# Routing tokens to experts tile by tile inside the stage before, in a two-block transformer kernel on one core

## The chip, the core and the metric

One Trainium2 core runs the whole program once. The number is the device time of that launch in microseconds, the median of the runs shown. The engines are TensorE (PE, with its weight loads PEld), VectorE (DVE), ScalarE (ACT), GpSimd (POOL) and SyncE (SP, which here only issues DMAs).

## What is computed

512 tokens of width 1024 pass through a first block (three groups of dilated window attention and a retention branch, merged by gates, an `out` product, then a mixture of experts) and two layers of a second block. The change is all between the `out` product and the experts. In the reference, cut to that:

```python
h = h + mix                                   # mix = merged @ w_out
hn = rms_norm(h, norm_moe_w)
g_w, g_idx = top_k(softmax(hn @ w_group + b_group), 1)        # 8 groups
sel = (hn @ w_expert + b_expert).reshape(T, 8, 8)[group g_idx]
e_w, e_idx = top_k(softmax(sel), 2);  e_w = e_w / sum(e_w)
gate = g_w * e_w;  eid = g_idx * 8 + e_idx                    # 2 of 64 experts a token
y[token] = sum over its 2 experts e of gate * ((silu(x @ w1[e]) * (x @ w3[e])) @ w2[e])
```

Each w1, w3, w2 is 2048 KB, so the 64 experts read 192 such arrays.

## The kernel before

Every engine runs its own instruction list, and semaphores order them. Tokens lie in four tiles of 128 (`NT` = 4). Between stages all engines meet at a barrier (`next_stage`): PE, VectorE and ScalarE drain, POOL clears the stage's semaphores and opens the next stage (L254).

**The rest stage** (`rest_pe`, `rest_dve`, `rest_act`) follows one list of steps, `rest_steps`, which all three engines walk, each taking the steps that concern it. Its last eight jobs are the `out` product: half 0 of the columns for tiles 0 to 3, then half 1. A job is 24 matmuls in 8 chunks. VectorE adds the result to `h`. After half 1 of a tile, ScalarE sums the squares and VectorE writes the normed tile (L1307, L357). `x_turn` transposes that tile (L1060) and ScalarE copies it to `xnT`; `logits` multiplies it by the routing weights (L1047, 72 columns) into PSUM bank 7. `logits` of a tile stands one job behind its `x_turn`, the last two behind all jobs.

**The routing stage** (`route_pe`, `route_dve`, `route_act`) stands between two barriers. VectorE works on all four tiles at once: bias, best group, the two best experts in it, gates; then `either`, the 0/1 matrix of tokens by experts. TensorE multiplies it by a triangle and by ones, which gives each token's rank in its expert and each expert's count. An expert has 32 slots (`CAP`); ranks beyond that go to spilled blocks, whose experts come from a running sum over the counts. VectorE works out each assignment's slot, counting the spilled ones too (L1503 to L1523).

**The expert stage.** `experts_dve` begins with 0/1 matrices: `picks` (which token is in which slot of a quad of four experts) and `gated` (the same times the gate), for quad 0, then `picks` for quad 1, then `spilled_experts_dve`. TensorE gathers quad 0's tokens by matmuls of `xn` with `picks` (L1608), ScalarE copies them to `xT`. Then 64 turns, one for each expert e (`body`): TensorE does the gate product and the up product of e (L1618), the down product of e - 1 (L1634), a transpose of `gated` (L1725), a quarter of the gather for a later quad, the transposes of gate and up (L1625) and adds a finished tile's results (L1654). VectorE copies `up` out of PSUM (L1785), copies half of the down result, sums the transposed gate and up, multiplies them, and writes `picks` and `gated` for later quads.

**The loads** (`experts_sp`, L1570): eight slots of 2048 KB hold weights: slots 0 to 3 are the ring that also holds the units of the `out` product, slot 4 is `xnT`, slot 5 the routing weights' rows, slots 6 and 7 the upper end of `arena`. Eight loads are issued ahead; load (e, j) after that waits until PE has used its slot: `pair_used` counts in the gate/up and down products, `down_used` in the transpose of `gated`. The ninth load, (2,2), waits for `pair_used` 1, which expert 0's first up matmul gives; the tenth, (3,0), for `pair_used` 2, given by the first matmul of the gather in expert 0's turn; the eleventh, (3,1), for `down_used` 2, in expert 1's turn.

## Time and profile before

| | us |
|---|---|
| median of 3 runs (lowest, highest) | 2969.37 (2968.95, 2972.18) |
| profiled execution, its own time | 2969.08 |
| its span in the trace | 2967.3 |
| TensorE busy, share of the span | 2701.6, 91% |
| VectorE busy | 1305.7, 44% |
| mean granted TensorE clock | 0.966 |
| bytes by DMA | 572.19 MB |

The page cuts the span into 40 slices of 74 us. For each it gives the busy share of the engines, the granted TensorE clock (1.00 is 2.4 GHz, 0.50 is 1.2 GHz) and the GB/s moved by DMA. A mean over the span says little here, since stages have different limits; so the page is read for where a stage lies and the windows, waits and timeline for what limits it. Times in the trace are counted from the start of the span.

### The profile page before, as it was taken

Reading aid. Unit: us, or ns where it says so; the run is one execution under the profiler, and the core shown is the slowest. Engines: PE = TensorE matmul, PEld = TensorE weight load, DVE = VectorE, ACT = ScalarE, POOL = GpSimd, SP = SyncE. Lnnn points to the kernel's source line nnn. Section 1 sums busy time; section 2 is a strip of 40 time slices with the busy share of each in tenths; the row PEclk is TensorE's granted clock in tenths of the full one; section 3 lists DMA queues with packets and bytes.
Section 4 is the critical chain, followed back from the end, with each engine's and each line's share of the span. In section 5 each row is a group of like instructions: output and inputs, shape, how many; then the busy total and the mean of one; then the engine's idle time right before and its main releaser. Section 6 shows DMA issues by size and latency. Waiting matters only on the chain.

```text
span 2967.3 us, 35548 instructions
## 1 busy us (share of the span) xinstructions
PE 2701.6 (91%) x14188; PEld 1911.8 (64%) x14188; DVE 1305.7 (44%) x2359; ACT 873.9 (29%) x1643; POOL 705.8 (24%) x310
## 2 busy tenths in 40 slices
PE   7999999998788888888888789999999999899998
PEld 7987777887433333333333277688788776788787
DVE  4333745324533333333333366454443574644433
ACT  3333334332111111111111143543332344433332
POOL 4232233442000000000000122224445122234443
PEclk9999999999899999999999899899999999999999
DMA  3222211325799999999999721022322221122321
GB/s 141 85 89 104 72 64 66 103 85 206 300 426 428 427 429 428 429 428 430 428 429 427 331 83 57 29 86 85 105 94 85 98 79 57 57 86 86 98 102 71
DMA packets 126801, 572.19 MB, mean 193 GB/s; under 512 B 10705, under 2 KB 58193, under 8 KB 101329
## 3 DMA queue, kind: packets, MB, share of 16 engines
q1 hardware_dynamic: 121424, 561.08, 47.6%
q10 hardware_dynamic: 5248, 9.32, 0.9%
q8 instruction: 90, 1.47, 0.2%
q14 instruction: 39, 0.31, 0.0%
HBM read 566.12 MB, written 4.26 MB: 192 GB/s over the span
## 4 chain that ended last, share of the span: by engine, by line
PE 50%; DMA 24%; PEld 9%; DVE 7%; issue 4%; ACT 3%; POOL 1%; PEldq 1%; POOLq 0%; SPq 0%; ACTq 0%; DVEq 0%
PE ps L341 27%; DMA wide<-in_moe_w 17%; PEld ps L341 9%; PE ps L1217 7%; DMA arena<-in_moe_w 6%; PE ps L1634 4%; PE ps L1618 3%; PE ps L555 1%; POOL ring_r L310 1%; PE ps L1026 1%; PE ps L526 1%; ACT ring_r L298 1%; PE ps L541 1%; PE ps L2548 1%; PE ps L1017 1%
## 5 line engine op out<-in xcount | busy, mean ns | idle before, releaser
L310 POOL TENSOR_TENSOR ring_r<-ring,ring_r 128x1024 fp32r<-128x1024 f32 (+2 forms) x284 | 690.8, 2464 | 2182.2 <-ACT ring_r L298 2182.2
L341 PE MATMUL ps<-xnT_r,ring_r 128*128 128x512 f32 (+1 forms) x1664 | 494.8, 378 | 13.1 <-DVE xn_r L2510 7.2
L341 PE MATMUL ps<-ring_r,xnT_r 128*128 128x512 f32 (+1 forms) x1360 | 443.8, 397 | 11.8 <-POOLq L254 5.0
L341 PEld LDWEIGHTS ps<-xnT_r,ring_r 128*128 128x128 f32 x1664 | 307.9, 191 | 79.8 <-issue 14.6
L341 PE MATMUL ps<-ring_r,arena_r 128*128 128x512 f32 x1392 | 334.1, 397 | 3.1 <-issue 3.1
L341 PEld LDWEIGHTS ps<-ring_r,xnT_r 128*128 128x128 f32 x1360 | 288.0, 224 | 59.2 <-issue 16.3
L341 PE MATMUL ps<-xn_r,ring_r 128*128 128x512 f32 (+1 forms) x832 | 312.6, 376 | 0.0
L341 PEld LDWEIGHTS ps<-ring_r,arena_r 128*128 128x128 f32 x1392 | 261.4, 190 | 68.1 <-issue 13.7
L1618 PE MATMUL ps<-wide,arena 128*32 128x512 f32 x1536 | 203.3, 652 | 101.4 <-DMA wide<-in_moe_w 100.9
L298 ACT ACTIVATE ring_r<-ring 128x1024 fp32r<-128x1024 f32 (+2 forms) x284 | 270.6, 1024 | 82.0 <-DMA ring<-in_w_down 68.0
L1618 PEld LDWEIGHTS ps<-wide,arena 128*32 128x32 f32 x1536 | 42.3, 112 | 239.4 <-DMA wide<-in_moe_w 146.9
L1634 PE MATMUL ps<-wide,arena 128*32 128x512 f32 x768 | 182.7, 619 | 0.0
L2808 DVE SCALAR_TENSOR_TENSOR arena<-ps,arena 128x511 f32<-128x511 f32 x88 | 66.0, 749 | 257.6 <-ACT arena L2824 257.6
L341 PEld LDWEIGHTS ps<-xn_r,ring_r 128*128 128x128 f32 x832 | 158.7, 191 | 26.7
L1648 ACT ACTIVATE arena<-ps 32x512 f32<-32x512 f32 x64 | 37.5, 586 | 469.1 <-PE ps L1634 469.1
L341 PE MATMUL ps<-ring_r,h_r 128*128 128x512 f32 (+1 forms) x424 | 167.7, 396 | 0.0
L1785 DVE COPY arena<-ps 128x512 f32<-128x512 f32 x64 | 44.3, 692 | 276.8 <-PE ps L1618 267.4
L2824 ACT ACTIVATE arena<-ps,arena 128x512 f32<-128x512 f32 x88 | 60.7, 690 | 299.9 <-PE ps L341 299.9
L1608 PE MATMUL ps<-arena,xn 128*128 128x128 f32 x1024 | 126.5, 278 | 14.6 <-DVE arena L1669 14.6
L1634 PEld LDWEIGHTS ps<-wide,arena 128*32 128x32 f32 x768 | 47.9, 117 | 135.2 <-issue 135.2
L1608 PEld LDWEIGHTS ps<-arena,xn 128*128 128x128 f32 x1024 | 124.6, 198 | 14.8 <-DVE arena L1669 14.8
L1629 DVE TENSOR_REDUCE arena<-ps 128x128 f32<-128x512 f32 x128 | 82.5, 686 | 109.9 <-PE ps L1625 109.7
(352 smaller groups left out, 3625.5 us busy)
## 6 DMA issues: line engine op xcount, KB each, us to landing
wide<-in_moe_w SPq DMA_DIRECT2D x144, 2048.0 KB, 27.0
arena<-in_moe_w SPq DMA_DIRECT2D x48, 2048.0 KB, 27.3
ring<-in_w_in SPq DMA_DIRECT2D x25, 2048.0 KB, 8.2
ring<-in_w_up SPq DMA_DIRECT2D x22, 2048.0 KB, 8.7
ring<-in_w_down SPq DMA_DIRECT2D x10, 2048.0 KB, 8.0
ring<-in_w_out SPq DMA_DIRECT2D x6, 2048.0 KB, 8.4
ring<-in_w_ret_branch SPq DMA_DIRECT2D x2, 2048.0 KB, 8.8
attn_spill<-arena ACTq DMA_DIRECT2D x2, 1056.0 KB, 10.8
```

What stands on the lines that cost most here:

```text
L298: nc.scalar.activation(ring_r[:, 2 + q % 2, cols], unit_home(q)[:, cols], ACT.Copy).then_inc(half_high, 1)
L310: nc.gpsimd.tensor_tensor(ring_r[:, q % 2, cols], ring[:, q % 2, cols], ring_r[:, 2 + q % 2, cols].bitcast(F32), ALU.subtract).then_inc(ha ...
L341: ins = nc.tensor.matmul(bank, left, right, start=(start and k == 0), stop=(stop and k == 2))
L1217: ins = nc.tensor.matmul(ps[:, job_bank(n), 0:right.shape[1]], left, right, start=(x == 0), stop=(x == len(pairs) - 1))
L1608: return [nc.tensor.matmul(ps[:, into, (c - c0) * width:(c - c0 + 1) * width], xn[:, i, c * P:(c + 1) * P], E.picks[:, quad, i, 0:width], ...
L1618: res.append(nc.tensor.matmul(ps[g * CAP:(g + 1) * CAP, bank, :], xT[:, c, :], w[:, c, :], start=(c < 4), stop=(c >= KC - 4), tile_positio ...
L1629: return nc.vector.tensor_reduce(dst, ps[:, bank, :].rearrange("p (c g k) -> p c k g", c=FC, g=4), AX.X, ALU.add)
L1634: return [nc.tensor.matmul(ps[half * CAP:(half + 1) * CAP, DOWN_BANK, :], E.hT[:, c, :], w[:, c, half * BANK:(half + 1) * BANK], start=(c ...
L1648: return nc.scalar.activation(E.y[expert_rows(b), b // QUAD % 2, 0:BANK], ps[0:CAP, DOWN_BANK, :], ACT.Copy)
L1785: nc.vector.tensor_copy(E.up, ps[:, UP_BANK, :]).then_inc(Z.up_kept, 1)
L2808: link(nc.vector.scalar_tensor_tensor(out=acc[:, 1:], in0=bank[:, 0:S - 1], scalar=taps[:, 1:2], in1=acc[:, 1:], op0=ALU.mult, op1=ALU.add))
L2824: nc.scalar.activation(Y.acc[:, j % 2, s_], ps[:, UP_BANKS[n % 8], :], ACT.Copy, scale=Y.fconv[:, s_ * FB + j, FCONV - 1:FCONV]).then_inc( ...
```

## The change

- The barrier between the rest stage and routing, and the one between routing and the experts, are gone; so is the stage `route`. Ranks, logits and gathers are steps of the rest stage's list.
- `route_tile_dve` finds group and experts of one tile. It sets the logits of other groups to -1e30 and searches all 64, where before the logits of the best group were cut out first. `place_tile_dve` gives the tile's main slots from its rank alone (a rank of 32 or more gets a slot far away) and writes its `picks`.
- `first_gather_pe` gathers quad 0 by tile, accumulated over the tiles in four PSUM banks.
- Gates, `gated` and the `picks` of quad 1 are made at the start of the expert stage. The slots of spilled assignments (`all_slots_dve`) come behind VectorE's turn for expert 1, `spilled_experts_dve`, in two halves, behind its turn for expert 2.
- SP issues (2,0) and (2,1) behind the first two loads; (1,1) and (1,2) wait for the last tile's logits to be read instead of the barrier.

```diff
 rest_steps, for n over the jobs from 2 * NT:
+                last = n - job_at("out", 1, 0)
                 for c in range(len(REST[n][1]) // 3):
                     yield "chunk", (n, c)
+                    if last == 2 and c == 3:   yield "logits", 0
+                    elif last == 2 and c == 5: yield "route", 0
+                    elif last == 3 and c == 3: yield "logits", 1
+                    elif last == 3 and c == 5: yield "route", 1
+                    elif last == 3 and c == 6: yield "x_turn", 2
...
-                after = n - job_at("out", 1, 1)
-                if after >= 1:
-                    yield "logits", after - 1
-                if after >= 0:
-                    yield "x_turn", after
-            yield "logits", NT - 2
-            yield "x_turn", NT - 1
-            yield "logits", NT - 1
+                if 1 <= last <= 2:
+                    yield "x_turn", last - 1
+            rank 0, rank 1, logits 2, x_turn 3, route 2, rank 2, logits 3, place 0, place 1,
+            gather 0, gather 1, route 3, rank 3, place 2, gather 2, place 3, gather 3
...
+        def rank_pe(pe, i):
+            pe.wait_ge(Z.chosen, i + 1)
+            for j in range(i):
+                matmul(rank_of(i), table("ones"), G.either[:, j, :], start=(j == 0), stop=False)
+            matmul(rank_of(i), table("before"), G.either[:, i, :], start=(i == 0), stop=True).then_inc(Z.ranked, 1)
+            if i == NT - 1:
+                for j in range(NT):
+                    ins = matmul(ps[:, COUNT_BANK, 0:EXPERTS], table("ones"), G.either[:, j, :], ...)
+                ins.then_inc(Z.ranked, 1)
...
+        def route_tile_dve(v, link, i):
+            v.wait_ge(Z.logits_ready, i + 1)
+            tensor_tensor(G.logits, ps[logits of i], G.bias, ALU.add).then_inc(logits_taken, 1)
+            v.wait_ge(logits_taken, i + 1)
+            link(max(G.best, lg));  link(max_index(G.best_at, G.best, lg))
+            tensor_tensor(E.num[:, i, :], lg, G.best[:, 0:1], ALU.subtract)
+            link(tensor_copy(G.group, G.best_at[:, 0:1]))
+            link(scalar_tensor_tensor(masked, erow[:, 0:EGROUPS], G.group[:, 0:1], ones, is_equal, subtract))
+            link(scalar_tensor_tensor(G.masked, G.masked, -NEG, G.logits[:, EGROUPS:], mult, add))
+            link(max(G.top, G.masked));  link(max_index(G.top_at, G.top, G.masked))
+            ins = tensor_tensor(E.one[:, i:i + 1], G.top[:, 1:2], G.top[:, 0:1], subtract)
+            if i == NT - 1: ins.then_inc(Z.exp_asked, 1)
+            link(tensor_copy(E.e_at[:, i, :], G.top_at[:, 0:2]))
+            link(tensor_scalar(G.first_is, erow, E.e_at[:, i, 0:1], None, is_equal))
+            scalar_tensor_tensor(G.either[:, i, :], erow, E.e_at[:, i, 1:2], G.first_is, is_equal, add).then_inc(Z.chosen, 1)
+        def place_tile_dve(v, link, i):
+            v.wait_ge(Z.ranked, max(i + 1, 2))
+            for k in range(2):
+                ins = scalar_tensor_tensor(G.chosen[:, k], expert_row, E.e_at[:, i, k:k + 1], rank_of(i), is_equal, mult)
+            link(ins)
+            link(tensor_reduce(E.rank_at[:, i, :], G.chosen, AX.X, ALU.add))
+            link(G.over = (rank_at >= CAP) * FAR);  link(G.over += rank_at)
+            link(E.main[:, i, :] = e_at * CAP + over)
+            link(pick_dve(v, E.main, i, E.picks[:, 0]))
+            pick_second_dve(E.main, i, E.picks[:, 0]).then_inc(Z.picks_ready, 1)
...
         def experts_sp(sp):
             load_expert(sp, 0, 0, 0)
             load_expert(sp, 0, 0, 2)
+            load_expert(sp, 2, 2, 0)
+            load_expert(sp, 2, 2, 1)
             sp.wait_ge(unit_used, FIRST_UNITS)
             load_expert(sp, 0, 0, 1)
             load_expert(sp, 1, 1, 0)
-            sp.wait_ge(stage_open, STAGES_BEFORE_EXPERTS - 1)
+            sp.wait_ge(logits_taken, NT)
             load_expert(sp, 1, 1, 1)
             load_expert(sp, 1, 1, 2)
-            load_expert(sp, 2, 2, 0)
-            load_expert(sp, 2, 2, 1)
...
+        def first_gather_pe(pe, i):
+            pe.wait_ge(Z.picks_ready, i + 1)
+            if i == 0: wait_taken(pe, len(REST) - 1)
+            for q in range(QUAD):
+                for c in (2 * q, 2 * q + 1):
+                    ins = matmul(ps[:, q, (c % 2) * P:(c % 2 + 1) * P], xn[:, i, c * P:(c + 1) * P], E.picks[:, 0, i, :], ...)
+                if i == NT - 1: ins.then_inc(Z.gathered, 1)
...
         def experts_dve(v, link):
+            v.wait_ge(Z.ranked, NT + 1)
+            tensor_copy(E.count, ps[:, COUNT_BANK, 0:EXPERTS])
+            E.nearer = E.main - P;  link(E.ahead = E.main - 2 * P);  gates_dve(v, link)
             for i in range(NT):
-                pick_dve(v, E.slot, i, E.picks[:, 0])
-                link(pick_gated_dve(E.slot, i, E.gated[:, 0]))
-                pick_second_dve(E.slot, i, E.picks[:, 0]).then_inc(Z.picks_ready, 1)
+                link(pick_gated_dve(E.main, i, E.gated[:, 0]))
                 add_second_dve(i, E.gated[:, 0]).then_inc(Z.gated_ready, 1)
                 v.wait_ge(Z.gated_ready, i + 1)
-            for i in range(NT):
-                pick_dve(v, E.nearer, i, E.picks[:, 1])
+                link(pick_dve(v, E.nearer, i, E.picks[:, 1]))
                 pick_second_dve(E.nearer, i, E.picks[:, 1]).then_inc(Z.picks_ready, 1)
-            spilled_experts_dve(v, link)
...
             def body(it, b):
...
+                if first and e == 1: all_slots_dve(v, link)
+                if first and e == 2: spilled_experts_dve(v, link)
```

## Rows read from the trace of the kernel before

**Rows 1.** The page: GB/s in 40 slices, and the chain's shares by engine

```profile
GB/s 141 85 89 104 72 64 66 103 85 206 300 426 428 427 429 428 429 428 430 428 429 427 331 83 57 29 86 85 105 94 85 98 79 57 57 86 86 98 102 71
...
PE 50%; DMA 24%; PEld 9%; DVE 7%; issue 4%; ACT 3%; POOL 1%; PEldq 1%; POOLq 0%; SPq 0%; ACTq 0%; DVEq 0%
```

**Rows 2.** Windows: stretch, its us, busy of each engine, clock, DMA share, GB/s

```profile
780.00:790.00 10.00, 10.00 (x81) 4.76 (x77) 4.70 (x13) 2.04 (x5) 0.00 (x0) 1.00 0.95 370
...
800.00:1660.00 860.00, 730.80 (x4503) 312.05 (x4499) 317.12 (x660) 120.02 (x293) 0.00 (x0) 0.96 1.01 428
```

**Rows 3.** Waits of PE, 800 to 1660 us: total, times, longest

```profile
PE ps L1618 <- DMA wide<-in_moe_w: 97.7, 44, 3.0
```

**Rows 4.** Timeline of SP: start, duration, engine, line, operation, count

```profile
774.42 0.33 SPq L1570 DMA_DIRECT2D wide<-in_moe_w  x1
...
785.56 1.29 SPq L1570 DMA_DIRECT2D wide<-in_moe_w  x3
...
795.55 0.33 SPq L1570 DMA_DIRECT2D wide<-in_moe_w  x1
```

**Rows 5.** Timeline, end of the out product, idle before and its releaser in brackets

```profile
714.98 0.69 DVE L1307 TENSOR_TENSOR h<-h,ps 128x512 f32<-128x512 f32 x1 [2.31 <-PE ps L1217]
...
723.06 0.69 DVE L1307 TENSOR_TENSOR h<-h,ps 128x512 f32<-128x512 f32 x1 [3.56 <-PE ps L1217]
...
725.49 1.99 DVE L357 SCALAR_TENSOR_TENSOR xn<-h,small,rows 128x1024 f32<-128x1024 f32 x1
...
728.58 1.04 PE L1060 MATMUL ps<-cst,xn 128*128 128x128 f32 x8
...
730.36 2.00 PE L1047 MATMUL ps<-rows,xnT 128*128 128x72 f32 x16 [0.74 <-ACT xnT L1067]
```

**Rows 6.** Timeline of DVE in the routing stage and in the expert prologue

```profile
733.32 0.46 DVE L1447 TENSOR_TENSOR arena<-ps,small 128x288 f32<-128x288 f32 x1 [5.84 <-POOLq L254]
...
734.30 0.16 DVE L1455 FIND_INDEX8 arena<-arena 128x8 uint32<-128x8 f32 x1
...
748.10 0.20 DVE L1439 TENSOR_SCALAR arena<-arena 128x64 f32<-128x64 f32 x1
748.33 0.20 DVE L1440 TENSOR_SCALAR arena<-arena 128x64 f32<-128x64 f32 x1
...
754.99 0.16 DVE L1523 TENSOR_SCALAR small<-small 128x8 f32<-128x8 f32 x1
...
763.91 2.29 DVE L1529 TENSOR_TENSOR arena<-small,cst 128x2048 f32<-128x2048 f32 x1
```

**Rows 7.** Timeline of DVE: the first instruction of picks for tiles 0 and 1

```profile
756.11 0.29 DVE L1666 TENSOR_SCALAR arena<-small 128x128 f32<-128x128 f32 x1 [0.96 <-POOLq L254]
...
757.53 0.29 DVE L1666 TENSOR_SCALAR arena<-small 128x128 f32<-128x128 f32 x1
```

**Rows 8.** Timeline of PE: first gather, expert 0's products, gather in its turn

```profile
761.62 9.53 PE L1608 MATMUL ps<-arena,xn 128*128 128x128 f32 x64 [14.57 <-DVE arena L1669]
...
771.62 3.64 PE L1618 MATMUL ps<-wide,arena 128*32 128x512 f32 x32 [0.47 <-ACT arena L1645]
...
775.36 1.95 PE L1608 MATMUL ps<-arena,xn 128*128 128x128 f32 x16
```

**Rows 9.** Windows around the changes of the granted clock (column before DMA share)

```profile
308.00:309.00 1.00, 1.00 (x9) 0.89 (x9) 1.00 (x1) 0.00 (x0) 1.00 (x1) 0.85 0.00 0
...
735.00:736.00 1.00, 0.00 (x0) 0.00 (x0) 0.93 (x6) 0.22 (x1) 0.00 (x0) 0.69 0.43 147
...
741.00:746.00 5.00, 5.00 (x25) 5.00 (x25) 0.00 (x0) 0.00 (x0) 0.00 (x0) 0.50 1.01 429
...
765.00:766.00 1.00, 1.00 (x6) 1.00 (x6) 1.00 (x1) 0.38 (x1) 0.00 (x0) 0.50 0.00 0
766.00:767.00 1.00, 1.00 (x11) 1.00 (x10) 0.96 (x2) 0.00 (x0) 0.00 (x0) 0.95 0.00 0
```

**Rows 10.** Timeline of PE ahead of the fall at 308.7

```profile
305.54 2.98 PE L555 MATMUL ps<-arena,rows 64*128 64x64 f32 x16
```

More of the change, by code:

```diff
@@ L1133, in rest_dve @@
                     turn_tile_dve(v, k, Z.out_kept, M.mT[0], M.mT[1], Z.out_low)
+                elif what == "route":
+                    route_tile_dve(v, link, k)
+                elif what == "place":
+                    place_tile_dve(v, link, k)
         def gated_tile_dve(v, link, half, i):
@@ new lines, in gates_dve, with all_slots_dve @@
+        def gates_dve(v, link):
+            v.wait_ge(V.exp_ready, 1)
+            link(nc.vector.tensor_reduce(gates[:, :, 0], E.num, AX.X, ALU.add))
+            link(nc.vector.scalar_tensor_tensor(out=gates[:, :, 0], in0=E.one, scalar=1.0, in1=gates[:, :, 0], op0=ALU.add, op1=ALU.mult))
+            link(nc.vector.reciprocal(gates[:, :, 0], gates[:, :, 0]))
+            link(nc.vector.tensor_tensor(gates[:, :, 1], gates[:, :, 0], E.one, ALU.mult))
+        def all_slots_dve(v, link):
+            erow = table("expert_row")
+            link(nc.vector.tensor_scalar(E.further, E.count, -1.0, None, ALU.add))
+            whole_blocks(link, E.further, E.further)
+            link(nc.vector.tensor_scalar(E.further, E.further, 0.0, None, ALU.max))
+            link(nc.vector.memset(E.zeros, 0.0))
+            link(nc.vector.tensor_tensor_scan(E.counted, E.further, E.zeros, 0.0, ALU.add, ALU.add))
+            link(nc.vector.tensor_tensor(E.first, E.counted, E.further, ALU.subtract))
@@ L1488, in route_dve @@
-            for k in range(2):
-                ins = nc.vector.tensor_tensor(G.is_expert[k], erow[:, None, :].to_broadcast([P, NT, EXPERTS]),
-                                              G.e_at[:, :, k:k + 1].to_broadcast([P, NT, EXPERTS]), ALU.is_equal)
-            link(ins)
-            nc.vector.tensor_tensor(G.either, G.is_expert[0], G.is_expert[1], ALU.add).then_inc(Z.chosen, 1)
-            erow2 = table("expert_row")
-            nc.vector.tensor_copy(E.columns[:, 0:EXPERTS], erow2)
@@ L1495, in route_dve @@
-            nc.vector.tensor_scalar(E.columns[:, EXPERTS:], erow2, float(EXPERTS), None, ALU.add)
-            v.wait_ge(Z.ranked, 1)
-            link(nc.vector.tensor_copy(G.count, ps[:, 6, 0:EXPERTS]))
-            for i in range(NT):
-                ins = nc.vector.tensor_copy(G.rank[:, i, :], ps[:, 4 + i % 2, (i // 2) * EXPERTS:(i // 2 + 1) * EXPERTS])
-            link(nc.vector.tensor_scalar(G.further, G.count, -1.0, None, ALU.add))
-            whole_blocks(link, G.further, G.further)
@@ L1503, in route_dve @@
-            link(nc.vector.tensor_scalar(G.further, G.further, 0.0, None, ALU.max))
-            link(nc.vector.memset(G.tmp, 0.0))
-            link(nc.vector.tensor_tensor_scan(E.counted, G.further, G.tmp, 0.0, ALU.add, ALU.add))
-            link(nc.vector.tensor_tensor(G.first, E.counted, G.further, ALU.subtract))
-            m = G.part
-            whole_blocks(link, m, G.rank)
-            link(nc.vector.scalar_tensor_tensor(out=G.place, in0=m, scalar=-float(CAP), in1=G.rank, op0=ALU.mult, op1=ALU.add))
@@ L1515, in route_dve @@
-            link(nc.vector.scalar_tensor_tensor(out=G.place, in0=G.by_group, scalar=float(CAP), in1=G.place, op0=ALU.mult, op1=ALU.add))
-            for k in range(2):
-                ins = nc.vector.tensor_tensor(G.is_expert[k], G.is_expert[k], G.place, ALU.mult)
-            link(ins)
-            for k in range(2):
-                ins = nc.vector.tensor_reduce(E.slot[:, :, k], G.is_expert[k], AX.X, ALU.add)
-            link(ins)
-            nc.vector.tensor_scalar(E.nearer, E.slot, -float(P), None, ALU.add)
@@ L1523, in route_dve @@
-            link(nc.vector.tensor_scalar(E.ahead, E.slot, -2.0 * P, None, ALU.add))
+            link(nc.vector.tensor_reduce(E.row, E.first_of, AX.X, ALU.add))
+            whole_blocks(link, E.block, E.rank_at)
+            link(nc.vector.scalar_tensor_tensor(out=E.row, in0=E.row, scalar=float(EXPERTS - 1), in1=E.e_at, op0=ALU.add, op1=ALU.subtract))
+            link(nc.vector.tensor_tensor(E.row, E.row, E.block, ALU.add))
+            link(nc.vector.scalar_tensor_tensor(out=E.row, in0=E.block, scalar=0.0, in1=E.row, op0=ALU.is_gt, op1=ALU.mult))
@@ L1664, in pick_dve @@
         def pick_dve(v, slots, i, dst, width=P):
[L1666 removed]
+            return nc.vector.tensor_scalar(dst[:, i, 0:width], E.columns[:, 0:width], slots[:, i, 0:1], None, ALU.is_equal)
         def pick_second_dve(slots, i, dst, width=P):
@@ L1815, in body @@
                     unite(it, b, e)
+                if first and e == 1:
+                    all_slots_dve(v, link)
+                if first and e == 2:
+                    spilled_experts_dve(v, link)
             turns(v, body)
```

242 lines of the change are left out of this document (133 added, 109 removed).

## Prediction

> **What bounds the kernel now.** I read the GB/s line of the page first: from slice 12 to slice 22 it stands at 426 to 430, nowhere else. That is the stage of the 64 experts, and the chain that ended last gives DMA 24% of the span [rows 1]. The windows of that stage show the transfers at 1.01 of all engines and 428 GB/s from 800 to 1660 us, with TensorE busy 731 of 860 us [rows 2]; the waits agree: TensorE's expert matmuls wait 98 us for weights in `wide` alone [rows 3]. A load is 2048 KB (2.097 MB), so 4.90 us at 428 GB/s, and three loads make an expert 14.7 us long. TensorE needs less: SP issues loads as the matmuls free their slots, and the issues at 785.56 and 795.55 us are 10.0 us apart for one expert [rows 4].
>
> So a time before this stage counts in one place only: when the unbroken stream of loads begins. Eight loads go out ahead. The ninth waits for expert 0's gate product (774.42 us), the eleventh for the transpose in expert 1's turn (785.56 us) [rows 4]. Two loads last 9.8 us from 774.42 to some 784.2, so DMA pauses about 1.3 us before the eleventh; the window 780 to 790 shows that as 0.95 [rows 2]. From the eleventh on it never pauses. **The eleventh issue, 785.56 us, is the anchor**: what moves it moves the end, until the two stages behind it, which the change doesn't touch.
>
> **What lies ahead of the anchor, before.** TensorE finishes the last out job at 723.0 (VectorE takes it at 723.06), the last normed tile ends at 725.49 + 1.99 = 727.5, its transposes (728.6) and logits (to 732.4) follow [rows 5], and a stage barrier lasts to 733.3. Then VectorE routes all four tiles at once, from 733.32 to 755.15, nothing beside it but the ranking matmuls, another barrier to 756.11 [rows 6, 7], four tiles of picks at 1.42 us, all 64 gather matmuls (761.62, 9.53 us), expert 0 at 771.62 [rows 7, 8]. This stretch is serial, so shortening it pays in full.
>
> **The change, part by part.** I rebuild the new chain from these rows.
>
> 1. Last out job. The logits and the transposes are the same matmuls as before, but logits 1 (2.0 us) and transposes 2 (1.04 us) now stand ahead of the end of job 3, behind job 3 before. 723.0 + 3.1 = 726.1. What is queued behind them is the add, square and norm of tile 3: 4.46 us as before (723.06 to 727.48), so normed at 730.6 [rows 5]. A cost of 3.1 us. Transposes 2 wait for no one: job 2 ends 2.0 us later than before (714.98, now 717.0), its norm 4.46 us behind that at 721.5, and TensorE asks for it at some 724.6. Routes 0 and 1 (below, 2.7 us) follow logits that end two or more chunks of 0.7 us and a transpose before the next add, at some 714.0 and 722.6: done by 716.7 and 725.3, ahead of the adds at 717.0 and 726.1. Free, with 0.3 and 0.8 us to spare.
>
> 2. Route of one tile on VectorE: eleven dependent steps, two of them index searches of two instructions each, three with an extra independent one. A dependent step of 64 elements takes 0.23 us start to start (748.10 to 748.33); the search's second half alone is 0.16 [rows 6]. 6 x 0.23 + 3 x 0.20 + 2 x 0.28 + about 0.16 for extras = 2.7 us. Not seen in the trace: the masked form with a per-partition scalar on strided operands; bounds 0.2 and 0.45 us a step, and I take 0.23, as similar 64 element steps. **Place** of one tile: two products out of PSUM, one reduction, three small steps, two picks: 0.36 + 0.28 + 0.60 + 0.32 + 0.35 = 1.9 us.
>
> 3. VectorE behind norm 3: route 2 (to 733.3), place 0, place 1 (to 737.1), route 3, place 2, place 3. 2 x 2.7 + 4 x 1.9 = 13.0 us, so picks at 743.6 if TensorE never keeps it waiting. Before, the same result took 733.32 to about 761.8. Both barriers (0.96 us each) go too, and so do the counting, the scan and the spilled slots.
>
> 4. TensorE in between: logits 2 in VectorE's norm, transposes 3, then idle until route 2 ends (1.6 us), rank 2 and logits 3, gathers 0 and 1, rank 3, gathers 2 and 3. A gather of one tile is 16 matmuls, 1.95 us at the full clock (775.36); only the last tile's stands behind the last pick. Full clock: gather 3 from 743.7 to 745.5, one copy of 0.4, expert 0 at 746.0.
>
> 5. **The clock.** The granted clock is at 2.4 GHz (1.00) ahead of this and fell to 1.2 GHz (0.50) at 735.4 (0.69 over that microsecond), when TensorE had stood since 732.4; ranking matmuls of 64 columns without a pause (741 to 746, 25 in 5.0 us) left it at 0.50, and the gather brought it back at 766.1. At 308.7 it fell too, and there TensorE had not paused at all: it had run sixteen 64x64 matmuls since 305.5 [rows 5, 9, 10]. The new stretch from 728.8 to 738 has two pauses (1.9 us to transposes 3, 1.6 to rank 2) with only transposes and narrow matmuls between. That is nearer to the two falls than to anything I see that kept the clock, so I take a fall near 733 and a return inside the gathers, near 743. Then: rank 2 in 1.3 (six at 0.2) and logits 3 in 3.6 us (between 2.0 and twice that), to 738.2, so route 3 starts 1.1 late and ends at 740.9; gathers 0 and 1 take 3.6 and 2.5, to 744.3; rank 3 (0.9) to 745.2; place 3 to 747.1; the count, gathers 2 and 3 and the copy to 750.4. Expert 0 at 750.4 against 771.62: 21.2 us early, and 25.6 with the clock held.
>
> The Trainium skill, TensorE: Matmul & The Clock Gate, "Why this matters for your kernels", has it that only a pause between bursts of matmuls longer than either of these brings the clock down. By that page the full-clock sum would hold; the row at 308.7, a fall without a pause, disagrees, and I follow the row.
>
> 6. What moves behind the last pick: VectorE's first duties in the expert stage (count, gates, gated picks of quad 0, picks of quad 1): 1.5 + 4 x 1.55 = 7.7 us, by the 1.42 of a five-instruction tile plus one link [rows 7]. Queued behind it: the gather for quad 1 in expert 0's turn, which TensorE reaches 3.74 us after expert 0 starts [rows 8]. 747.1 + 7.7 = 754.8 against 754.1: **a new wait of 0.7 us** (1.6 at full clock, and up to 3 if the block takes 10). Net: 21.2 - 0.7 = **20.5 us**; 25.6 - 1.6 = 24.0 with the clock held.
>
> 7. Slots for all blocks behind expert 1, some 27 steps: 8 products, 15 dependent steps of 0.2 to 0.23, a 512 element reduction 0.7, scan 0.3: 5.8 us. Spilled blocks behind expert 2: four 1024 element steps, half of the 2.29 us row each, and three small ones: 5.1 us [rows 6]. Their cover: VectorE rests in each 10 us turn. Queued behind them is the copy of `up`, which slips from 791.96 to about 796.6 (in before's frame) while TensorE turns it only at 797.7. Cost 0 to 0.5 us a turn, and the stream has 10.0 + 4.7 = 14.7 us per turn to take it from. If the cover is gone: up to 5 us each less the 4.7 of slack that a turn leaves, some 3 in all. Nothing below zero: no transfer is taken away.
>
> 8. Loads. SP's order puts (2,0), (2,1) behind the first two, at 696.6; (0,1) waits for the last out job as before and lands by 726.1 + 2 x 4.9 + 2 = 738, wanted at 748 or later. (1,1), (1,2) wait for the fourth logits (738.2), land by 749, wanted after 757. Hidden at both places; behind them in SP's queue is the ninth load, which is due later still. Exp on ScalarE: one table load, under route 3. POOL loses two barriers and had nothing to do.
>
> **Sum.** Anchor 785.56 - 20.5 = 765.1 us. The profiled execution took 2969.08 us (span 2967.3); the median of three is 2969.37, 0.3 above it. 2969.08 - 20.5 + 0.3 for the median = 2948.9, say **2949.0 us**.
>
> **Rivals.**
> - *Clock held* (the page's rule): 24.0 us, **2945.4 us**. For it: each pause is shorter than the 3.0 us before the fall at 735.4. Against it: 308.7.
> - *Longer chain*: the VectorE steps cost 0.27 instead of 0.23 (13.0 becomes 15.3), or the clock comes back only with expert 0, which puts rank 3 at 1.7 and the last two gathers at 3.6 each, +4.5; or the inserts of step 7 cost their 3. **2951.5 to 2956.5 us**.
> - *The change doesn't do what it says*: the gathers wait for everything as before (a bank or slot that comes free late) and only the barriers and the counting fall away, 2 to 6 us: within 0.2%, **2965 us**.
> - *Slower*: TensorE stays at 1.2 GHz into the experts. A turn of 10.0 us of almost unbroken matmuls becomes 19, 4.3 us over the stream's 14.7. It undoes the gain of 20.5 after five such turns and is slower by over 0.2% (5.9 us) after seven: **2975 us or more**. Against it: gathers and gate products are what brought the clock back in 4.5 us at 761.6, and the windows from 800 to 1660 show 0.96.
>
> **How the numbers follow.** Forecast (2946.5 to 2951.5) 0.53, clock held 0.20, longer chain 0.20, not what it says 0.03, slower 0.04. The range takes in the first three: 2943.5 (held, with steps at 0.20 us) to 2956.0. What a measurement of this kernel can tell from no change is about 0.2%, 5.9 us. Faster 0.93, same 0.03, slower 0.04.
>
> **What would show it.** Eleventh issue near 765; expert 0's first gate product near 750; a granted clock of 0.5 between some 733 and 743 (by its absence the held rival); logits 3 in 3 to 4 us; route of a tile 2.7, place 1.9; windows from 790 on at 1.01 and 428 GB/s; the `up` copies of turns 2 and 3 late on VectorE but TensorE's turns not longer than 10.5 us. Wrong would be: DMA below 0.95 anywhere between 775 and 1640, or a gap between expert 0's up product and its gather of over 3 us.

## The result, and the profile after

| | before | after |
|---|---|---|
| median, us (lowest to highest, runs) | 2970.77 (2968.95 to 2973.34, 4) | 2950.52 (2947.89 to 2951.01, 4) |
| ratio, 95% interval | | 0.9929 (0.9912 to 0.9947) |
| profiled execution, its span | 2969.08, 2967.3 | 2951.01, 2949.2 |
| add of out job 3 on VectorE | 723.06 | 725.79 |
| expert 0's first gate product | 771.62 | 749.21 |
| eleventh load issued (the anchor) | 785.56 | 764.13 |
| load of `in_gate_bias`, the first that waits for the experts' end | 1703.80 | 1682.32 |
| from there to the end | 1263.5 | 1266.9 |

The kernel is 20.2 us faster (2970.77 - 2950.52). The page of the profile after, GB/s in 40 slices and the chain, answers [rows 1]:

```profile
GB/s 141 86 87 107 72 65 57 112 87 228 378 427 428 428 429 428 429 428 429 428 429 427 285 65 58 56 60 112 88 86 107 99 58 58 57 86 86 103 97 72
...
PE 50%; DMA 24%; PEld 10%; DVE 7%; issue 4%; ACT 3%; POOL 1%; PEldq 0%; POOLq 0%; SPq 0%; ACTq 0%; DVEq 0%
```

Slice 11, in which the experts begin, moves 378 GB/s instead of 300, and slice 23, in which they end, 285 instead of 331: the same bytes, earlier. Timeline of TensorE in the profile after, from the logits of tile 2 on (start, duration, instructions, in brackets the idle time before and what ended it), beside [rows 5, 8]:

```profile
726.57 1.96 PE L1076 MATMUL ps<-rows,xnT 128*128 128x72 f32 x16
730.23 1.09 PE L1090 MATMUL ps<-cst,xn 128*128 128x128 f32 x8 [1.70 <-DVE xn L358]
733.08 1.12 PE L1472 MATMUL ps<-arena,cst 128*128 128x64 f32 x4 [1.76 <-DVE arena L1515]
...
734.42 3.63 PE L1076 MATMUL ps<-rows,xnT 128*128 128x72 f32 x16
737.85 5.52 PE L1729 MATMUL ps<-arena,xn 128*128 128x128 f32 x32
...
744.94 3.79 PE L1729 MATMUL ps<-arena,xn 128*128 128x128 f32 x32
749.21 3.64 PE L1659 MATMUL ps<-wide,arena 128*32 128x512 f32 x32 [0.47 <-ACT arena L1686]
752.78 0.33 PE L1773 MATMUL ps<-cst,arena 128*128 128x128 f32 x1
753.83 2.05 PE L1649 MATMUL ps<-arena,xn 128*128 128x128 f32 x16 [0.73 <-DVE arena L1710]
```

The logits of tile 2 take 1.96 us and those of tile 3, the same sixteen matmuls, 3.63: the clock fell between them. Windows of the same profile (us, busy of PE, PEld, DVE, ACT, POOL, granted clock, DMA share, GB/s) show when, and what the loads do once the experts run, beside [rows 2, 9]:

```profile
730.00:731.00 1.00, 0.77 (x7) 0.78 (x8) 0.87 (x7) 0.08 (x1) 0.00 (x0) 1.00 1.08 459
731.00:732.00 1.00, 0.32 (x3) 0.08 (x1) 0.89 (x5) 1.00 (x2) 0.00 (x0) 0.62 0.92 393
732.00:741.00 9.00, 7.92 (x37) 7.92 (x38) 7.08 (x36) 1.61 (x4) 0.00 (x0) 0.50 0.79 297
741.00:742.00 1.00, 1.00 (x9) 1.00 (x9) 0.93 (x5) 0.00 (x0) 0.00 (x0) 0.76 1.04 442
...
762.00:772.00 10.00, 10.00 (x77) 4.76 (x75) 5.86 (x21) 2.04 (x5) 0.00 (x0) 1.00 0.86 328
780.00:800.00 20.00, 18.95 (x138) 9.07 (x130) 13.98 (x29) 4.09 (x10) 0.00 (x0) 1.00 1.00 427
800.00:1640.00 840.00, 708.48 (x4357) 302.20 (x4357) 307.67 (x635) 115.81 (x283) 0.00 (x0) 0.96 1.01 428
```

The pause of DMA ahead of the eleventh load is now in the window 762 to 772; behind it nothing is missing. The issue itself, in SP's timeline beside [rows 4]:

```profile
764.13 10.32 SPq L1611 DMA_DIRECT2D wide<-in_moe_w  x4
```

VectorE's timeline, beside [rows 6, 7]: the last out add, norm 3, first and last instruction of route 2, the starts of place 0, route 3 and place 3, the first step of the spilled slots and of the spilled blocks, each with the copy of `up` behind it:

```profile
725.79 0.69 DVE L1341 TENSOR_TENSOR h<-h,ps 128x512 f32<-128x512 f32 x1 [0.67 <-PE ps L1251]
...
728.22 1.96 DVE L358 SCALAR_TENSOR_TENSOR xn<-h,small,rows 128x1024 f32<-128x1024 f32 x1
730.02 0.21 DVE L1497 TENSOR_TENSOR arena<-ps,small 128x72 f32<-128x72 f32 x1
...
732.74 0.28 DVE L1515 SCALAR_TENSOR_TENSOR arena<-cst,small,arena 128x64 f32<-128x64 f32 x1
732.95 0.47 DVE L1524 SCALAR_TENSOR_TENSOR arena<-cst,small,ps 128x64 f32<-128x64 f32 x2
...
738.09 0.23 DVE L1497 TENSOR_TENSOR arena<-ps,small 128x72 f32<-128x72 f32 x1 [1.05 <-PE ps L1076]
...
744.25 0.47 DVE L1524 SCALAR_TENSOR_TENSOR arena<-cst,small,ps 128x64 f32<-128x64 f32 x2 [1.12 <-PE ps L1473]
...
769.35 0.20 DVE L1545 TENSOR_SCALAR arena<-arena 128x64 f32<-128x64 f32 x1
...
775.50 0.69 DVE L1830 COPY arena<-ps 128x512 f32<-128x512 f32 x1
...
779.89 1.23 DVE L1570 TENSOR_TENSOR arena<-small,cst 128x1024 f32<-128x1024 f32 x1
...
785.53 0.69 DVE L1830 COPY arena<-ps 128x512 f32<-128x512 f32 x1
```

**Where the time went.** From the add of job 3 to the eleventh load lie 38.34 us (before 62.50); the add comes 2.73 us later, so the anchor moved by 24.16 - 2.73 = 21.43 us. TensorE's last wait for an expert's load and the load of `in_gate_bias` moved by 21.50 and 21.48: the stream carried the gain through unchanged. But the span is only 18.1 us shorter. The missing 3.4 us are in code that the change doesn't touch (1263.5 us before, 1266.9 after).

### The profile page after: what moved, and what is told of

The parts are those of the page before. It is cut to its first block, busy times and chain, and to the rows that moved or that the text cites. A ratio compares the mean times of both kernels' runs of the same rounds, so it can differ in the third digit from the quotient of the medians.

```text
span 2949.2 us, 35577 instructions
## 1 busy us (share of the span) xinstructions
PE 2702.1 (92%) x14188; PEld 1914.1 (65%) x14188; DVE 1314.7 (45%) x2403; ACT 873.3 (30%) x1643; POOL 707.1 (24%) x310
## 4 chain that ended last, share of the span: by engine, by line
PE 50%; DMA 24%; PEld 10%; DVE 7%; issue 4%; ACT 3%; POOL 1%; PEldq 0%; POOLq 0%; SPq 0%; ACTq 0%; DVEq 0%
PE ps L342 27%; DMA wide<-in_moe_w 17%; PEld ps L342 10%; PE ps L1251 7%; DMA arena<-in_moe_w 6%; PE ps L1675 4%; PE ps L1659 3%; PE ps L556 2%; POOL ring_r L311 1%; PE ps L1049 1%; PE ps L527 1%; ACT ring_r L299 1%; PE ps L542 1%; PE ps L2589 1%; PE ps L2597 1%
## 5 line engine op out<-in xcount | busy, mean ns | idle before, releaser
L2847 DVE TENSOR_TENSOR arena_r<-arena,arena_r 128x512 fp32r<-128x512 f32 x44 | 72.9, 1676 | 130.6 <-ACT arena_r L2843 130.6
L1251 PE MATMUL ps<-ring_r,xnT_r 128*128 128x512 f32 x384 | 125.1, 396 | 3.0 <-POOLq L255 1.7
```

The lines of the kernel that those rows point to most:

```text
L1251: ins = nc.tensor.matmul(ps[:, job_bank(n), 0:right.shape[1]], left, right, start=(x == 0), stop=(x == len(pairs) - 1))
L2847: nc.vector.tensor_tensor(Y.act_low[:, b], Y.act[:, b], Y.act_high[:, b % HIGH_BLOCKS].bitcast(F32), ALU.subtract).then_inc(Z.act_low, 1)
```

## The experiments

In the profiles I read four lengths: from job 3's add to expert 0 (**E0**), from that add to the eleventh load (**L11**), from the eleventh load to TensorE's wait for the last expert's second load (**stream**), and from the load of `in_gate_bias` to the end (**tail**); last the time in the tail at a granted clock of 0.50, without the last fall, which comes when TensorE has no work left. The first three leave out when the add itself comes, which is told apart below.

| kernel | add | E0 | L11 | stream | tail | at 0.50 |
|---|---|---|---|---|---|---|
| before | 723.06 | 48.56 | 62.50 | 891.3 | 1263.5 | 85.3 |
| after | 725.79 | 23.42 | 38.34 | 891.3 | 1266.9 | 95.6 |
| after_again | 728.82 | 23.35 | 38.29 | 891.5 | 1262.7 | 81.9 |
| after_third | 730.77 | 23.33 | 38.26 | 891.3 | 1263.5 | 88.7 |
| e2_warm | 728.12 | 20.84 | 36.06 | 891.6 | 1262.6 | 81.9 |
| e3_prologue | 728.03 | 23.44 | 37.37 | 891.3 | 1262.8 | 75.1 |
| e8_warm_prologue | 730.80 | 21.67 | 35.61 | 891.5 | 1262.7 | 81.9 |
| e9_warm_picks | 728.00 | 20.85 | 34.78 | 891.4 | 1256.2 | 68.3 |
| e1_spill_ahead | 728.82 | 24.03 | 50.52 | 891.2 | 1263.0 | 85.3 |
| e4_two_more | 730.95 | 23.41 | 38.34 | 892.0 | 1262.8 | 81.9 |
| e5_four_more | 729.15 | 23.97 | 38.90 | 902.6 | 1263.1 | 85.3 |
| e6_loads_late | 728.64 | 23.47 | 38.41 | 895.7 | 1262.1 | 75.1 |
| e7_gather_last | 725.91 | 28.61 | 42.54 | 891.5 | 1259.3 | 71.7 |

Five kernels ran once only: e2_warm 2946.91 us, e3_prologue 2946.55, e4_two_more 2952.85, e6_loads_late 2953.51, e7_gather_last 2948.01. These times decide nothing: e7_gather_last comes out below the changed kernel although its L11 is 4.2 us longer. The lengths do: E0, L11 and stream repeat within 0.2 us in three profiles of the changed kernel.

**after_again, after_third: the changed kernel once more.** No edit.

> The changed kernel once more, unchanged, to see what of its time is the stage it changes. In the first profile of it the eleventh load is issued at 764.13 us, 21.4 us earlier than before, and the expert stage ends 21.5 us earlier, yet the span is only 18.1 us shorter: 3.4 us are lost in the two layers behind, whose code is the same, where the clock stood at 0.50 for 10 us longer. Theory A (the clock's falls in the layers differ from run to run): the eleventh load within 1 us of 764.1 again, and the time from the expert stage's end to the end anywhere between 1263 and 1267 us, the longer the more of it is at 0.50. Theory B (the change causes it, by something it leaves behind): again 1266.5 to 1267.5 us behind the experts.

> The changed kernel, unedited, on the same chip as e9_warm_picks. Expert 0 23.4 us and the eleventh load 38.3 us behind job 3's add; the expert stage from the eleventh load to the last load wait 891.3; job 3's add anywhere from 725 to 731 us, the time behind the experts 1259 to 1267.

Medians 2950.0 (ratio 0.9926, 0.9912 to 0.9941) and 2950.88 (0.9933, 0.992 to 0.9947). E0, L11 and stream repeat; the tail falls back to 1262.7 and 1263.5. So the 3.4 us lost in the tail belong to that one execution, not to the change, as far as two more profiles can tell. What was missed in after_again is the anchor's own time, 767.11 instead of about 764: the add came 3 us later. In the twelve profiles of the new order the add lies anywhere from 725.79 to 730.95, and the granted clock goes with it: with 10.2 us at 0.50 ahead of the add it comes at 725.79 and 725.91, with 13.7 at 728.00 to 728.12, with 17.1 at 728.64 to 729.15, with 20.5 at 730.77 to 730.95. Half of the 10.2 us that lie between the first and the last group is 5.1 us, about the 5.2 by which the adds differ. The windows show some of these falls, in after and then in after_third, in work that no kernel here changes:

```profile
322.00:327.00 5.00, 5.00 (x33) 3.99 (x33) 4.25 (x7) 0.00 (x0) 0.00 (x0) 1.00 0.00 0
385.00:413.00 28.00, 27.82 (x134) 22.91 (x132) 6.91 (x18) 7.86 (x12) 7.44 (x4) 0.94 0.19 71
```

```profile
322.00:327.00 5.00, 5.00 (x24) 3.61 (x25) 4.07 (x7) 0.00 (x0) 0.00 (x0) 0.66 0.00 0
385.00:413.00 28.00, 26.47 (x111) 21.48 (x112) 8.67 (x21) 7.24 (x13) 3.94 (x2) 0.82 0.22 76
```

Why the clock falls more often in one execution of the same code than in another stays open. After and before can be compared, because both have 10.2 us at 0.50 ahead of the add: the adds of job 0, three jobs ahead, stand at 702.30 and 702.51 in them, and those of job 3 23.49 and 20.55 us behind. The difference of 2.94 is the cost of logits 1 and transposes 2 in between.

**e2_warm: hold the clock.** Adds four matmuls that nobody reads (eight records in the trace), two in each of the pauses ahead of `x_turn` 3 and of rank 2:

```diff
+        def keep_warm(n):
+            matmul(ps[bank of the last out job, 0:n], table("before"), cst[:, 0:n], start=True, stop=True)
 x_turn 3 in rest_pe:
+            wait_taken(pe, job_at("out", 1, 2));  keep_warm(512);  keep_warm(256)
             turn_tile_pe(...)
+            keep_warm(512);  keep_warm(256)
```

> Adds four matmuls whose result nobody reads (128x512 and 128x256 in each of TensorE's two pauses, behind logits 2 and behind transposes 3; some 1.4 us of dense work in pauses of 1.7 and 1.8 us). Theory (the narrow matmuls and pauses bring the clock down, and TensorE is what ends last in the stretch from 737.9 to 748.7): the clock stays at 1.00 from 700 to 760, logits 3 takes 2.0 us instead of 3.63, the four gathers 1.9 us each, VectorE becomes what ends last, expert 0 starts at 746.5 instead of 749.2, the wait ahead of its gather grows from 0.9 to some 1.5, the eleventh load comes at 762.0 instead of 764.1. Rival (the fall has another cause, or the clock's price is hidden behind VectorE's chain): eleventh load within 0.5 us of 764.1. Since the clock falls at different moments of a run, a fall in spite of the added work is possible; then logits 3 stays above 3 us and the eleventh load at 764.

The clock stayed at 1.00. TensorE's timeline of e2_warm:

```profile
733.53 1.46 PE L1088 MATMUL ps<-cst 128*128 128x512 f32 x4
735.46 0.66 PE L1482 MATMUL ps<-arena,cst 128*128 128x64 f32 x4 [0.48 <-DVE arena L1525]
...
736.18 1.96 PE L1083 MATMUL ps<-rows,xnT 128*128 128x72 f32 x16
...
753.88 2.05 PE L1659 MATMUL ps<-arena,xn 128*128 128x128 f32 x16 [1.02 <-DVE arena L1720]
```

Logits 3 are back at 1.96 us and expert 0 starts 2.6 us earlier, but the wait for the picks of quad 1 grew from 0.73 to 1.02, so that L11 gains 2.3. The clock costs the change 2.3 us of L11. The added matmuls also shorten the two pauses, to 0.40 and 0.48 us; whether that or the added work as such held the clock is not told apart.

**e3_prologue: take the new wait away.** Nothing is added; VectorE makes the gates ahead of place 3 and all picks of quad 1 behind the first gated matrix:

```diff
 place of the last tile in rest_dve:
+                    if k == NT - 1: gates_dve(v, link)
                     place_tile_dve(v, link, k)
 experts_dve:
-            gates_dve(v, link)
             for i in range(NT):
                 link(pick_gated_dve(E.main, i, E.gated[:, 0]));  add_second_dve(i, ...)
-                link(pick_dve(v, E.nearer, i, E.picks[:, 1]));  pick_second_dve(E.nearer, i, ...)
+                if i == 0:
+                    for k in range(NT): pick_dve(..., k, ...);  pick_second_dve(..., k, ...)
```

> Only the order of VectorE's work: the gates move into its pause of 1.1 us ahead of place 3, and the picks of quad 1 come behind the first gated tile, ahead of the other three. Theory (TensorE's gather in expert 0's turn waits 0.9 us for these picks, and that wait lies on the path to the eleventh load): the wait is gone, the gather starts at 749.2 + 3.7 = 752.9 instead of 753.83, the eleventh load comes at 763.2 instead of 764.1, the rest is the same. Rival (the wait is hidden): 764.1 as before.

The wait is gone: TensorE's gather for quad 1 in e3_prologue follows its transpose at once,

```profile
755.04 0.33 PE L1775 MATMUL ps<-cst,arena 128*128 128x128 f32 x1
755.21 1.95 PE L1651 MATMUL ps<-arena,xn 128*128 128x128 f32 x16
```

L11 is 0.97 us shorter than in after. So the new wait's price is 0.9 to 1.0 us.

**e8_warm_prologue: both edits at once.**

> Both edits at once: the four added matmuls in TensorE's pauses and the new order of VectorE's prologue. Theory: 2.7 us from the clock at expert 0's start and no wait ahead of its gather, so the eleventh load at 764.1 - 3.6 = 760.5 us, and a time some 3.6 us below the changed kernel's, 0.12%, which is inside what a timed comparison can tell; the row of the eleventh load decides. Rival (loads, not this chain, set the eleventh issue): no earlier than 763.

Median 2947.1 (0.9919, 0.9905 to 0.9933). L11 fell by 2.7 against after, not by 3.6. TensorE's timeline of e8_warm_prologue shows the lost microsecond inside the gathers:

```profile
749.95 2.05 PE L1741 MATMUL ps<-arena,xn 128*128 128x128 f32 x16 [0.79 <-DVE arena L1722]
```

The gather of tile 3 waits 0.79 us for its picks. In e3_prologue the gates filled VectorE's pause of 1.12 us ahead of place 3; with the clock held, rank 3 is ready sooner and VectorE has no pause ahead of place 3 (nor has it in e2_warm), so the gates lie on the path.

**e9_warm_picks: e8_warm_prologue with the gates back at the head of the expert stage.** It keeps e2's unread matmuls and e3's order of the picks; the edit against e8_warm_prologue:

```diff
 place of the last tile in rest_dve:
-                    if k == NT - 1: gates_dve(v, link)
 experts_dve:
+            gates_dve(v, link)
```

> Adds to the changed kernel the dense matmuls of e2_warm, which nobody reads, and makes all picks of quad 1 behind the gated matrix of tile 0, as e3_prologue does, but leaves the gates at the head of the expert stage, where e8_warm_prologue had moved them onto the path. Theory (e8's lost microsecond is the gates in a pause that is gone): expert 0 starts 20.8 us behind job 3's add, as in e2_warm; the gather in its turn waits for nobody (3.7 us behind expert 0's start), the turn takes 6.6 us; the eleventh load is issued 35.1 us behind job 3's add, 3.2 less than in the changed kernel, and the first load behind the experts 953.5 us behind it. Rival (the gates were not it; the reordered picks themselves delay something): expert 0 21.7 behind the add as in e8_warm_prologue, or the gather in expert 0's turn still waits 0.5 us or more. Median against the changed kernel in the same call: 3 us less by the theory, 2 by the rival, each with some 2 us of spread from where the last out job ends and from the clock behind the experts.

Median 2944.02 (2939.16 to 2947.86; ratio 0.9916, 0.9903 to 0.993), after_third, measured beside it, 2950.88. TensorE's timeline of e9_warm_picks and SP's eleventh issue:

```profile
748.85 3.64 PE L1669 MATMUL ps<-wide,arena 128*32 128x512 f32 x32 [0.47 <-ACT arena L1696]
752.42 0.33 PE L1783 MATMUL ps<-cst,arena 128*128 128x128 f32 x1
752.58 1.95 PE L1659 MATMUL ps<-arena,xn 128*128 128x128 f32 x16
```

```profile
762.78 1.28 SPq L1621 DMA_DIRECT2D wide<-in_moe_w  x3
```

E0 20.85, L11 34.78: both edits now count, 3.5 us together, and e8's loss was the gates. The rival, that the reordered picks delay something, falls. Of the 6.9 us between the medians the lengths give these 3.5 to the edit. The rest is not shown to be the edit's: its profile has the shortest tail of all, 1256.2 us, and the two intervals overlap. By L11 it is the best version found.

**e1_spill_ahead: the slots and blocks of the spilled at the head of the stage,** where the kernel before had them:

```diff
 experts_dve, behind the picks of quad 1:
+            all_slots_dve(v, link);  spilled_experts_dve(v, link)
 body:
-                if first and e == 1: all_slots_dve(v, link)
-                if first and e == 2: spilled_experts_dve(v, link)
```

> Undoes one part: the slots of all blocks and the spilled blocks are worked out in the prologue again, behind the picks of quad 1 and ahead of expert 0's turn on VectorE, instead of behind the turns of experts 1 and 2. They take 6.2 and 5.6 us there. Theory (what stands ahead of the eleventh load is paid in full): the copy of up in turn 0 comes at 765.5 instead of 753.7, TensorE waits about 10 us for it in the transposes of turn 0, the eleventh load is issued at 774.0 instead of 764.1, and the time is 9.9 us longer than the changed kernel's, some 2960.5. Rival (TensorE's or the loads' slack absorbs it, since eight loads lie ready): eleventh load within 1 us of 764, time as the changed kernel's.

Median 2957.65 (0.9948, 0.9932 to 0.9965). TensorE's timeline of e1_spill_ahead:

```profile
769.87 1.13 PE L1666 MATMUL ps<-cst,arena 128*128 128x128 f32 x4 [9.86 <-DVE arena L1832]
770.93 4.70 PE L1659 MATMUL ps<-wide,arena 128*32 128x512 f32 x32
```

L11 grew by 12.2, 2.3 more than expected. Turn 0 is 10.5 us longer (18.08 against 7.58), as thought. But the wait of 9.86 us also took the clock down (0.50 at 763), and expert 1's gate and up products took 4.70 us instead of 3.64: 1.1 us. The first gathers, too, ran 0.7 us longer than in after_again (6.13 and 5.44), because the first fall came later against them; that is not the edit's. So moving these steps behind the experts' work is worth some 11.5 us of L11, about half of the whole gain. The median shows less of it, 7.1 us over the changed kernel's, with intervals that overlap: the profile is the slowest of four executions (2951.89 to 2962.28). Why the other executions lose less is not shown.

**e4_two_more and e5_four_more: how much VectorE work a turn hides.** They repeat the spilled blocks (5.1 us by my estimate, 5.64 measured) two and four times more behind expert 2:

```diff
                 if first and e == 2:
                     spilled_experts_dve(v, link)
+                    for _ in range(2):            # 4 in e5_four_more
+                        spilled_experts_dve(v, link)
```

> Two further passes instead of four: 11.3 us of VectorE work more behind turn 2. Theory: 11.3 is below the 14.3 us of slack, so the stream doesn't pause, the expert stage ends at the same time as in the changed kernel (first of the loads behind the stage's end at 1682.3 us, within 0.5 us). Rival (VectorE's turns are on the path): 11 us later.

> Four further passes of the spilled blocks' steps behind turn 2 (the same result each time), 22.6 us of VectorE work more at the same place. Theory (the loads' stream has slack there): turn 3's transpose of up waits some 22 us; the first load that this delays is the twentieth, (6,1), whose slot was free at 793.95 while the stream comes to it at 764.1 + 9 x 4.9 = 808.2, 14.3 us later. So 22.6 - 14.3 = 8.3 us are lost once, DMA below 1.00 for that long between 800 and 820, and the time is 8.3 us longer than the changed kernel's, 2959. Rival (VectorE's turns are on the path): 22 us longer, 2972.

Two more, 11.3 us of VectorE time, lengthen the stream by 0.7 us; four more by 11.3 us (median 2958.1, 0.9953, 0.9936 to 0.997). So in the profiles there is slack of about the size I gave, and it ends. The median is 7.6 us over the changed kernel's, and here, too, the profiled execution is the slowest of its four. e4_two_more's load of `in_gate_bias` comes 0.8 us later behind the eleventh load than in after, where I had expected at most 0.5. The stream of e5_four_more grew by 3.0 us more than the expected 8.3; its timeline and windows show where most of that comes from:

```profile
812.79 1.13 PE L1666 MATMUL ps<-cst,arena 128*128 128x128 f32 x4 [22.36 <-DVE arena L1830]
813.85 5.52 PE L1659 MATMUL ps<-wide,arena 128*32 128x512 f32 x32
```

```profile
810.00:815.00 5.00, 2.21 (x12) 1.13 (x16) 4.73 (x10) 0.31 (x1) 0.00 (x0) 0.50 0.78 331
815.00:820.00 5.00, 5.00 (x32) 1.17 (x26) 2.17 (x9) 0.60 (x1) 0.00 (x0) 0.73 0.02 5
820.00:825.00 5.00, 5.00 (x34) 2.85 (x31) 0.82 (x2) 0.71 (x2) 0.00 (x0) 1.00 0.32 56
```

The long wait lowered the clock, which made the turn behind it 1.9 us longer (5.52 instead of 3.64). That leaves 1.1 us of the excess, which I can't place. The loads already issued carry DMA to 814; then its share lacks 9.4 us in three windows (22, 98 and 68% of 5 us each).

**e6_loads_late: (2,0) and (2,1) issued behind (1,2) again, as before the change.**

```diff
 experts_sp:
-            load_expert(sp, 2, 2, 0);  load_expert(sp, 2, 2, 1)
             sp.wait_ge(unit_used, FIRST_UNITS)
...
             load_expert(sp, 1, 1, 2)
+            load_expert(sp, 2, 2, 0);  load_expert(sp, 2, 2, 1)
```

> Undoes one part: the loads (2,0) and (2,1) come last of the eight again, behind the wait for the fourth logits at 738. Theory (the start of the unbroken stream is what counts): four loads instead of two follow that wait, so the ninth and tenth wait in the queue behind them, and the eleventh, still issued at 764.1, starts its transfer only when 6 x 4.9 us of loads from 738.2 have passed, at 767.6; the pause of DMA before the eleventh goes, and the expert stage ends 3.5 us later, at 1685.8 instead of 1682.3. Rival (the order is free, since nobody waits for (2,0) before 766): the same end within 0.5 us.

L11 is unchanged (38.41), and the stream 4.4 us longer. Windows behind the eleventh issue (767.1 in both), first e6_loads_late, then after_again:

```profile
767.00:777.00 10.00, 10.00 (x76) 4.76 (x75) 7.62 (x28) 2.05 (x6) 0.00 (x0) 1.00 1.00 424
```

```profile
767.00:777.00 10.00, 10.00 (x75) 4.76 (x75) 7.64 (x28) 2.05 (x6) 0.00 (x0) 1.00 0.92 351
```

DMA is busy without a pause here, since it still owes the loads that went out late. The anchor holds only while DMA reaches it with nothing left to do.

**e7_gather_last: all gathers behind the last pick,** accumulated by tile as in the change:

```diff
 rest_steps:
-            gather 0, gather 1, route 3, rank 3, place 2, gather 2, place 3, gather 3
+            route 3, rank 3, place 2, place 3, gather 0, gather 1, gather 2, gather 3
```

> Undoes one part: all four gathers of quad 0 stand behind place 3 on TensorE, instead of between the routes and places. Theory (the gathers by tile take TensorE's idle time, and keep its clock from staying low): TensorE waits from 738.0 to route 3's end at 740.9, ranks at the lower clock until 744.4, then gathers; the first at 3.6 us, the clock returns some 4.5 us into them, the last ends at 754; expert 0 starts at 754.5 instead of 749.2, the wait ahead of its gather goes (0.9), and the eleventh load comes at 768.5 instead of 764.1. Rival (TensorE's work is hidden behind VectorE's chain either way): 1.9 x 3 us less what TensorE waited, at most 1 us later.

E0 +5.2, L11 +4.2: the new wait, which expert 0 now reaches later, is gone and gives 1 us back. TensorE's timeline of e7_gather_last:

```profile
741.31 1.55 PE L1472 MATMUL ps<-arena,cst 128*128 128x64 f32 x6 [3.13 <-DVE arena L1515]
...
744.79 9.26 PE L1729 MATMUL ps<-arena,xn 128*128 128x128 f32 x64
```

Doing the gathers in VectorE's shadow is worth 4.2 us. Part of that is the clock: without them TensorE has a longer pause, 3.13 us, and seventeen microseconds at the low clock (0.51 on average from 732 to 749) instead of ten.

No run puts the barriers or the routing of all four tiles at once back, so what each of these two gives alone is not shown.

## Why the prediction was right, and where it was off

**The anchor held.** I forecast 2949.0; it is 2950.5, a gain of 20.2 us. The eleventh load goes out at 764.13 (765.1 forecast) and the end of the stage follows it exactly: the stream is 891.3 us in before and in after, and 891.2 to 891.6 in every kernel that leaves the loads and the turns behind the anchor alone. A net gain of 21.4 us stands against the 20.5 of my sum. Two things that the forecast left out move the time of each execution: when job 3's add comes (5.2 us over twelve profiles of the new order) and how long the tail is. Both go with the time at 0.50. The medians of the changed kernel, each against the before measured beside it, differ by 20.2, 21.2 and 19.2 us. That the forecast lies within 1.5 us is partly luck: in the sum itself dearer VectorE steps and a low clock that ended earlier worked against each other (steps 2 to 5).

**Step 1.** The inserts cost 2.94 us (3.1 forecast). The norm ends at 730.18 (730.6). Routes 0 and 1 cost nothing, but the 0.3 us to spare at route 0 weren't there: TensorE ends job 2 at 716.59, and VectorE takes it only at 716.83, straight behind route 0. Nobody waits for that tile before transposes 2 at 724.02. Ahead of the add of job 3 VectorE waits 0.67 us (0.8 forecast).

**Step 2.** A route takes 3.0 us, not 2.7. The steps on 64 elements that I had put at 0.23 us start to start take 0.26 to 0.32 (the longest is the masked one, L1505, whose operands no row of before had); the small ones take the 0.20 I had. Place takes 2.0 to 2.1 us, 1.9 forecast. The terms were mis-sized by 0.3 us for each route and 0.1 to 0.2 for each place.

**Steps 3 to 5.** The clock case was right in kind: 0.50 from 731.3 to 741.5 (forecast 733 to 743), logits 3 3.63 us (3.6). But it fell when the transposes behind the first pause ended, 1.7 us before my forecast, and so came back earlier too, in the first gathers: 5.52 us (6.1 forecast), done at 743.4 (744.3). This is why expert 0 starts at 749.21 and not 750.4, although VectorE's steps were dearer. What I called the held clock is worth 2.3 us at the anchor (e2_warm); I had priced it at 3.5 (24.0 against 20.5): expert 0 started only 2.6 us earlier (4.4 forecast), since by then VectorE's dearer steps set the pace.

The rule of the Trainium skill that the prediction weighed (TensorE: Matmul & The Clock Gate, "Why this matters for your kernels": only a pause longer than either of these between bursts lowers the clock) doesn't hold here. The clock fell in all nine profiles of the new order without added matmuls, each time either right behind the one pause of 1.7 us and the transposes or within the next pause, and in none of the three with them. The advice of the same page of the Trainium skill, "Loop structure matters more than you think", to leave no long waits between matmuls so that the clock stays up, agrees with e2_warm: clock 1.00, with 0.40 and 0.48 us left of the two pauses.

**Step 6.** The new wait exists: the gather for quad 1 waits 0.73 us for the picks (0.7 forecast), and taking it away gives 0.9 to 1.0 us.

**Step 7.** Slots 6.15 us (5.8), blocks 5.64 (5.1); the copy of `up` slips to 775.50 and 785.53, as told. The turns stay at 10.16 and 10.03 us, the stream doesn't lengthen: cost nothing, and e4_two_more shows that 11 us more would have cost only 0.7. What I mis-sized is the price without cover. I had "3 in all" for a turn whose cover is gone; with the work ahead of expert 1's turn it is some 11.5 us in the profile of e1_spill_ahead, where nothing ahead of the anchor absorbs it and the wait itself lowers the clock.

**Step 8.** "Hidden at both places" was wrong for (2,0) and (2,1), in the change's favour: left in their old place they cost 4.4 us (e6_loads_late). I asked only when each load is wanted, not whether DMA would be through with all eight when the stream begins. My sum of 20.5 contained this silently, because it took the pause ahead of the anchor for given.

**The 3.4 us in the tail.** Windows from 796 us behind the start of the tail, after and before, inside a layer that neither kernel touches:

```profile
2478.00:2488.00 10.00, 10.00 (x25) 5.98 (x25) 3.07 (x6) 3.32 (x10) 0.00 (x0) 0.66 0.44 181
2488.00:2498.00 10.00, 10.00 (x36) 6.85 (x34) 3.62 (x10) 3.64 (x8) 0.00 (x0) 0.66 0.00 1
```

```profile
2499.50:2509.50 10.00, 10.00 (x29) 5.42 (x27) 3.77 (x8) 3.80 (x11) 0.00 (x0) 0.83 0.36 150
2509.50:2519.50 10.00, 10.00 (x47) 6.80 (x47) 5.71 (x22) 6.00 (x14) 0.00 (x0) 1.00 0.00 0
```

At 1.00 TensorE does 47 instructions in ten microseconds, at 0.66 it does 36. Over the thirteen profiles the shortest tail has the least time at 0.50 (1256.2 us, 68.3) and the longest the most (1266.9, 95.6); between 75.1 and 88.7 it stays at 1262.1 to 1263.5 in no strict order. Ten microseconds more at 0.50, as between after and before, can cost at most five, so the clock suffices for the 3.4; that it is the whole cause is argued from these windows and not tested. Why the same code spends 82, 89 or 96 us at the low clock from one execution to the next stays open.

## What to carry to other kernels

Where loads limit a long stage, find the issue behind which the stream never pauses: everything ahead of it counts in full, work moved behind it is free up to the slack of a turn, and the forecast holds only if DMA reaches that issue with nothing left to do, so check the loads issued ahead of it as well. When steps alternate between TensorE and another engine, price TensorE's part at the half clock, and consider unread matmuls in its pauses. A step moved into a pause is free only as long as that pause exists: with the clock held, the gates that had been free in it cost 0.8 us.
